# Attention with the value products turned over and GpSimd scaling the probabilities

## The reference

```
h = rms_norm(x, g)
proj = h @ w_in                            # queries, keys, values, gates
o_a = dilated_attention(...)               # 4 heads, 3 groups of keys under one softmax
o_b = sliding_window_gqa(...)              # 8 heads, softmax with a sink
o_c = stick_breaking_attention(...)        # 4 heads, no softmax
merged = g0*(o_a @ w_br_a) + g1*(o_b @ w_br_b) + g2*(o_c @ w_br_c)
x = x + rms_norm(merged @ w_out)
x = x + rms_norm(conv_ffn(rms_norm(x)))
# then, twice:
oa = neighbourhood_attention(...)          # 8 heads, softmax
ob = sliding_window_gqa_2(...)             # 8 heads, softmax with a sink
x = x + (g0*(oa @ w_branch_na) + g1*(ob @ w_branch_swa)) @ w_out
x = x + peer_ffn(rms_norm(x))              # 16 experts of 16384 for each of 8 heads
```

## Time and profile before

| | us |
|---|---|
| median of 3 runs | 2282.3 |
| lowest and highest | 2281.91, 2283.56 |
| span of the profiled execution | 2280.1 |
| PE busy | 2025.5 |
| DVE busy | 1598.8 |
| ACT busy | 1144.3 |
| POOL busy | 821.2 |

### The profile page before, as it was taken

One profiled execution on the slowest core, in us unless ns is written; L12 is line 12 of the kernel. 1 busy time (PEld: TensorE's weight loads), 2 busy tenths in 40 slices (PEclk: granted clock), 3 DMA queues, 4 the chain that ended last, 5 costly groups with the idle time before them and its releaser, 6 DMA issues.

```text
span 2280.1 us, 29665 instructions
## 1 busy us (share of the span) xinstructions
PE 2025.5 (89%) x9846; PEld 1333.5 (58%) x9846; DVE 1598.8 (70%) x3217; ACT 1144.3 (50%) x2531; POOL 821.2 (36%) x531
## 2 busy tenths in 40 slices
PE   9999999999999998888877878999999887778787
PEld 8998899998898744432222223898744432223222
DVE  4565777777676887777677765676887777677774
ACT  4454455555454555444444445454555544454443
POOL 0000000000010255565666663010256566765754
PEclk9999999999999999999999999999999999999999
DMA  7544456655735899999999997634899999999998
GB/s 244 168 122 131 137 163 186 191 180 149 235 120 163 329 421 421 421 421 421 420 421 422 419 422 318 230 121 148 320 421 421 421 421 422 421 422 411 422 422 339
DMA packets 120771, 707.22 MB, mean 310 GB/s; under 512 B 13664, under 2 KB 13920, under 8 KB 55008
## 3 DMA queue, kind: packets, MB, share of 16 engines
q0 software_dynamic: 73728, 536.90, 56.7%
q1 hardware_dynamic: 43488, 157.63, 21.8%
q10 hardware_dynamic: 3456, 11.40, 1.4%
HBM read 704.84 MB, written 1.05 MB: 310 GB/s over the span
## 4 chain that ended last, share of the span: by engine, by line
PE 40%; DMA 24%; POOL 11%; DVE 9%; issue 9%; ACT 7%; POOLq 0%; DVEq 0%; ACTq 0%
DMA work<-in_experts,expert_idx 23%; POOL work L1071 11%; PE ps L547 10%; PE ps L549 10%; PE ps L548 10%; PE ps L1296 6%; PE ps L697 2%; DVE weights_lo L532 2%; DVE work L2126 2%; PE ps L675 1%; ACT weights_hi L527 1%; ACT L1586 1%; ACT L1637 1%; PE ps L665 1%; DVE work L2103 1%
## 5 line engine op out<-in xcount | busy, mean ns | idle before, releaser
L1296 PE MATMUL ps<-work,arena 128*128 128x512 f32 x2040 | 995.2, 620 | 211.4 <-ACT arena L1642 210.6
L1071 POOL DMA_INDIRECT work<-in_experts,expert_idx x512 | 796.9, 1556 | 735.8 <-PE ps L1296 290.5
L1296 PEld LDWEIGHTS ps<-work,arena 128*128 128x128 f32 x2040 | 360.5, 192 | 820.1 <-ACT arena L1642 524.5
L2126 DVE CUSTOM_DVE_ANT_0 work<-h_norm,work 128x1024 f32<-128x1024 f32 x480 | 588.2, 1226 | 332.6 <-DMA work<-in_experts,expert_idx 328.8
L532 DVE TENSOR_TENSOR weights_lo<-weights,weights_hi 128x1024 fp32r<-128x1024 f32 x280 | 347.4, 1246 | 183.0 <-ACT weights_hi L527 181.8
L547 PE MATMUL ps<-feat_hi,weights_hi 128*128 128x256 f32 x1576 | 459.4, 291 | 8.7 <-DVE weights_lo L532 5.8
L1637 ACT ACTIVATE small<-small 128x1 f32<-128x1 f32 x512 | 150.3, 293 | 609.2 <-DVE small L2126 587.2
L527 ACT ACTIVATE weights_hi<-weights 128x1024 fp32r<-128x1024 f32 x280 | 295.3, 1056 | 316.2 <-PE ps L549 271.0
L548 PE MATMUL ps<-feat_lo,weights_hi 128*128 128x256 f32 x1576 | 446.7, 283 | 0.0
L549 PE MATMUL ps<-feat_hi,weights_lo 128*128 128x256 f32 x1576 | 446.7, 283 | 0.0
L547 PEld LDWEIGHTS ps<-feat_hi,weights_hi 128*128 128x128 f32 x1576 | 302.9, 192 | 18.4 <-issue 8.5
(11 more groups left out here) (242 smaller groups left out, 1760.3 us busy)
## 6 DMA issues: line engine op xcount, KB each, us to landing
weights<-in_wstream SPq DMA_DIRECT2D x280, 512.0 KB, 4.2
work<-in_experts,expert_idx POOLq DMA_INDIRECT x512, 14.6
arena<-in_wstream SPq DMA_DIRECT2D x12, 512.0 KB, 5.7
arena<-in_na_bias ACTq DMA_DIRECT2D x6, 512.0 KB, 4.1
params<-in_wstream SPq DMA_DIRECT2D x6, 512.0 KB, 5.4
arena<-in_bias ACTq DMA_DIRECT2D x5, 512.0 KB, 4.4
params<-in_par ACTq DMA_DIRECT2D x2, 576.0 KB, 5.6
params<-in_par ACTq DMA_DIRECT2D x1, 1024.0 KB, 6.2
```

The source lines that it names most:

```text
L1071: nc.gpsimd.indirect_dma_start(ring[:, r, :], None, experts, bass.IndirectOffsetOnAxis(ap=EIDX[:, b, c * RING + r:c * RING + r + 1], axis= ...
L1296: ins = nc.tensor.matmul(bank(2 * t + h), DIAG[:, r, :], ring[:, r, D + h * 512:D + (h + 1) * 512], start=False, stop=False)
L2126: nc.vector.tensor_tensor_reduce(ring[:, r, 0:D], HN[:, t, :], ring[:, r, 0:D], 1.0, 0.0, ALU.mult, ALU.add, hd[:, r:r + 1]).then_inc(dots ...
```

## The change

Value products are turned over: the 64 columns of values are stationary and 128 columns of transposed probabilities move. The result is feature-major, 64 rows for a head; the even head of a pair goes to partitions 0 to 63, the odd one to 64 to 127, alternating. O becomes OT, feature-major, and the turns of heads go. Of the batches before the last two, DVE copies the heads to OT, and ACT and DVE make FH and FL from OT at "O" (three pairs of chunks in the first block, two in a layer). For the last two batches ACT and DVE make FH and FL from PSUM.

Not the heads are scaled but the probabilities, before they are transposed: at the new step "N" (for a batch and a half) DVE waits for the exponentials of that half and takes the reciprocals of the sums, and GpSimd multiplies the half in place. PE's transposes wait for GpSimd's halves. The order becomes N(b-1, 0), S(b), V(b-2), N(b-1, 1), G, T, G, T. In the last steps a product of the branches ("F") moves ahead of the last transposes, and ACT's sigmoid of the gates moves to the place of "F", ahead of the last batch's heads. The diff's core:

```diff
-        O, w0 = carve(work, w0, TT, D)
+        OT, w0 = carve(work, w0, KC, S)
...
+            far = (min(4 * fills[-1] + 4, b.blocks) - 1) // per >= b.n // 2
+            pe.wait_ge(A.probs, 2 * (l * A.batches + b.at) + (2 if far else 1))
+            transposes_pe(pe, A, b.fill, [b.L[:, r, k * P:(k + 1) * P] for r in range(b.n) for k in range(per)], l, fills)
...
-            pe.wait_ge(A.pTt, l * A.fills + b.fill + b.copies)
             out = bank(4 + b.values % 2)
-            for r, (_, vals) in enumerate(b.rows):
-                for k, v in enumerate(vals):
-                    ins = nc.tensor.matmul(out[:, r * HD:(r + 1) * HD], PT[:, r * per + k, :], v,
-                                           start=k == 0, stop=k == per - 1)
+            for j in range(b.n // 2):
+                pe.wait_ge(A.pTt, l * A.fills + b.fill + max(b.copies - 1, -(-(2 * j + 2) * per // 4)))
+                for k in range(per):
+                    for side in range(2):
+                        r = 2 * j + side
+                        ins = nc.tensor.matmul(out[side * HD:(side + 1) * HD, j * P:(j + 1) * P], b.rows[r][1][k], PT[:, r * per + k, :],
+                                               start=k == 0, stop=k == per - 1)
...
-            if half:
-                ins.then_inc(A.probs, 1)
+            ins.then_inc(exps_ready, 1)
+
+        def normed_dve(dve, ch, A, b, half, l=0):
+
+            if b.kind != "softmax":
+                return
+            r0, r1 = half * b.n // 2, (half + 1) * b.n // 2
+            dve.wait_ge(exps_ready, A.soft_before + 2 * (l * A.batches + b.at) + half + 1)
+            nc.vector.reciprocal(rsum[b.turn][:, r0:r1], sums[b.turn][:, r0:r1]).then_inc(inverse_ready, 1)
+
+        def normed_pool(pool, A, b, l=0):
+
+            if b.kind != "softmax":
+                return
+            for half in range(2):
+                r0, r1 = half * b.n // 2, (half + 1) * b.n // 2
+                part = b.L[:, r0:r1, 0:b.width]
+                wait_alone(pool, inverse_ready, A.soft_before + 2 * (l * A.batches + b.at) + half + 1, pool_passed)
+                nc.gpsimd.tensor_tensor(part, part, view(rsum[b.turn][:, r0:r1], [1, r1 - r0], [0, b.width]), ALU.mult).then_inc(A.probs, 1)
...
-            if b.kind == "softmax" and fills[0] == 0:
-                ch.step(nc.vector.reciprocal(rsum[b.turn][:, 0:b.n], sums[b.turn][:, 0:b.n]))
+
+        def heads_of(b):
+
+            return slice(b.col // P, b.col // P + b.n // 2), slice(b.q * P, (b.q + 1) * P)
+
+        def heads_out(b):
+
+            return bank(4 + b.values % 2)[:, 0:b.n * HD].rearrange("p (c n) -> p c n", n=P)
+
+        def heads_act(act, A, b, l=0):
+
+            act.wait_ge(A.pTr, l * A.fills + b.values + 1)
+            nc.scalar.activation(FH[:, *heads_of(b)], heads_out(b), ACT.Copy).then_inc(heads_hi, 1)
 
         def heads_dve(dve, ch, A, b, l=0):
-            n = b.values
-            dve.wait_ge(A.pTr, l * A.fills + n + 1)
-            dst, src = O[:, b.q, b.col:b.col + b.n * HD], bank(4 + n % 2)[:, 0:b.n * HD]
-            if b.kind == "softmax":
-                ch.sync()
-                nc.vector.tensor_tensor(dst.rearrange("p (n d) -> p n d", n=b.n), src.rearrange("p (n d) -> p n d", n=b.n),
-                                        view(rsum[b.turn], [1, b.n], [0, HD]), ALU.mult).then_inc(A.pTt, 1)
+
+            if b.direct:
+                dve.wait_ge(heads_hi, A.hi_before + l * (A.early + 2) + A.early + b.direct)
+                nc.vector.tensor_tensor(FL[:, *heads_of(b)], heads_out(b), FH[:, *heads_of(b)], ALU.subtract).then_inc(A.pTt, 1)
             else:
-                nc.vector.tensor_copy(dst, src).then_inc(A.pTt, 1)
+                dve.wait_ge(A.pTr, l * A.fills + b.values + 1)
+                nc.vector.tensor_copy(OT[:, *heads_of(b)], heads_out(b)).then_inc(A.pTt, 1)
...
+        def straight(batches):
+
+            batches[-2].direct, batches[-1].direct = 1, 2
+
+        def heads_parts(eng, A, b, l=0):
+
+            for f in range(A.early):
                 if eng is nc.scalar:
-                    eng.wait_ge(A.pTr, l * A.fills + n + 1)
-                    nc.scalar.activation(two(FH, f), src, ACT.Copy).then_inc(heads_hi, 1)
+                    eng.wait_ge(A.pTt, l * A.fills + b.fill)
+                    nc.scalar.activation(two(FH, f), two(OT, f), ACT.Copy).then_inc(heads_hi, 1)
                 else:
-                    eng.wait_ge(heads_hi, l * 4 + (0 if A is AT1 else 4) + f + 1)
-                    nc.vector.tensor_tensor(two(FL, f), src, two(FH, f), ALU.subtract).then_inc(A.pTt, 1)
-
...
-        def early_heads_pe(pe, A, b, taken, l=0):
-
-            pe.wait_ge(*taken)
-            pe.wait_ge(A.pTt, l * A.fills + b.fill)
-            turn_heads(pe, A, b.fill + b.fills, l, range(EARLY))
+                    eng.wait_ge(heads_hi, A.hi_before + l * (A.early + 2) + f + 1)
+                    nc.vector.tensor_tensor(two(FL, f), two(OT, f), two(FH, f), ALU.subtract).then_inc(heads_lo, 1)
...
+                past = batches[b.at - 1]
+                order += [("N", past, 0), ("S", b)] + ([("V", batches[b.at - 2])] if b.at > 1 else []) + [("N", past, 1)] + turned(past)
+            return order + [("N", batches[-1], 0)]
...
-            return [("V", b), ("O", b), ("T", last, range(last.copies)), ("P", b), ("V", last)]
+            c = last.copies
+            middle = [("T", last, range(1, c - 1))] if c > 2 else []
+            return [("N", last, 1), ("O", b), ("V", b), ("T", last, range(1)), ("P", b)] + middle + [("F", b), ("T", last, range(c - 1, c)), ("V", last)]
...
+            for b in batches1:
+                normed_pool(pool, AT1, b)
...
+                for b in batches2:
+                    normed_pool(pool, AT2, b, l)
...
-            gates_act(3 * KC, (proj_taken, IN_QKV + IN_GATE))
+                elif what[0] == "F":
+                    gates_act(3 * KC, (proj_taken, IN_QKV + IN_GATE))
+                elif what[0] == "V" and what[1].direct:
+                    heads_act(act, AT1, what[1])
...
-                if what[0] in "GSP":
+                if what[0] in "GSO":
```

More of the change, by code:

```diff
@@ L68 @@
 QKW = QK_HEADS * HD
-EARLY = 2
 ROWS = 4
@@ L608, in build, with __init__ @@
         class Attn:
-            def __init__(self, low, scores, logits, probs, pTr, pTt, batches, fills):
-                self.low, self.scores, self.logits, self.probs = low, scores, logits, probs
+            def __init__(self, low, scores, logits, soft_before, probs, pTr, pTt, batches, fills, early, hi_before, lo_before):
+                self.low, self.scores, self.logits, self.soft_before, self.probs = low, scores, logits, soft_before, probs
+                self.early, self.hi_before, self.lo_before = early, hi_before, lo_before
                 self.pTr, self.pTt = pTr, pTt
@@ L764, in stick_dve @@
             mask = before[:, S - w:S]
-            nc.vector.tensor_tensor(b3, b3, view(mask, [0, b.n], [1, w]), ALU.mult).then_inc(A.probs, 1)
-        def heads_first(batches):
-            batches[-1].behind_heads = True
-            batches[-1].fill += EARLY
-            batches[-1].values += EARLY
-        def heads_parts(eng, A, fill, l, fills):
-            for f in fills:
-                n = fill + f
-                src = bank(6 + f if f < EARLY else 4 + n % 2)
+            dve.wait_ge(A.probs, 2 * b.at)
@@ L815, in branches_pe @@
         def branches_pe(pe, A, fill, g0, parts, l=0, at=0):
-            pe.wait_ge(A.pTt, l * A.fills + fill + EARLY)
-            turn_heads(pe, A, fill, l, range(EARLY, 4))
-            first_branch(pe, 2 * g0 + 2, 3, 0, parts[0], at)
-            pe.wait_ge(A.pTt, l * A.fills + fill + 4)
+            pe.wait_ge(heads_lo, A.lo_before + (l + 1) * A.early)
+            pe.wait_ge(A.pTt, l * A.fills + fill)
             for g in range(BR):
@@ L996, in build @@
         rest2 = attention(batches2)
-        order2 += rest2[:2] + [("Q", 1, range(0, 2)), ("Q", 1, range(2, 3))] + rest2[2:] + last_steps(batches2)
+        behind = rest2.index("G") + 1
+        order2 += rest2[:behind] + [("Q", 1, range(0, 2)), ("Q", 1, range(2, 3))] + rest2[behind:] + last_steps(batches2)
         assert order2.count("G") == L_PROJ + L_GATE
@@ L1566, in _ @@
                     elif what[0] == "O":
-                        heads_parts(nc.scalar, AT2, what[1].fill + what[1].fills, l, range(EARLY))
-                gates_act(2 * KC, (lproj_taken, l * N2 + L_PROJ + L_GATE))
+                        heads_parts(nc.scalar, AT2, what[1], l)
+                    elif what[0] == "F":
+                        gates_act(2 * KC, (lproj_taken, l * N2 + L_PROJ + L_GATE))
+                    elif what[0] == "V" and what[1].direct:
+                        heads_act(act, AT2, what[1], l)
                 merge_act(act, AT2, fill_o2, G_LAYER + LG_BR, l, at)
@@ L1721, in _ @@
                 elif what[0] == "O":
-                    heads_parts(nc.vector, AT1, what[1].fill + what[1].fills, 0, range(EARLY))
```

(9 more changed lines are left out.)

58 lines of the change are left out of this document (24 added, 34 removed).

## The result

| | before | after |
|---|---|---|
| median of 5 runs, us | 2282.87 | 2265.74 |
| lowest and highest | 2281.91, 2283.56 | 2264.86, 2269.29 |
| span of the profiled execution | 2280.1 | 2263.9 |

The ratio is 0.9927, with a 95% interval of 0.9914 to 0.9939. That is faster by 17.1 us; by the two spans it is 16.2 us. The forecast was 2267.

What follows compares the result with a forecast made beforehand. PE was taken to bound attention's steady part, a chain through DVE and ACT its tails. -14.0 + 1.4 + 0.7 - 2.4 - 1.1 = -15.4 us from 2280.1, plus 2.2 around the span, gave 2267 us; own range 2262 to 2277.

Steps and rivals of the forecast that it cites:

- the forecast's first three terms: Attention's steady part: value products -14.0 us, mode changes +1.4 and the slackless place +0.7.
- Value products, -14.0: Steady attention: two products side by side in the array's halves save 0.0565 us for each of 248 records, 14.0 us.
- Mode changes, +1.4: Nine steady batches of values between row-tiled scores and full-height products: 0.15 us each, bounds 0 to 0.35, +1.4 us.
- Slackless place, +0.7: After a layer's first scores PE waits for DVE's copies; extra reciprocal and contention add 0.35 us, +0.7 for two layers.
- GpSimd's half, 2.5 us: GpSimd's multiplication of half a batch, at most 128 x 1024, takes 2.5 us, upper end 4.1; hidden in the steady part.
- Layer tails, -1.2 each: Each layer's tail: first product needing all heads at 706.7 instead of 707.87 us, 1.2 us earlier, -2.4 for two.
- First block: Its tail, ending behind ACT's sigmoid: -1.1 us; its narrowest half, 512 elements, ready some 0.5 us before PE's transposes.
- the second rival: The array's halves take turns in the value products: 2284.5 us, or 2281 without mode changes; chance 0.17.
- GpSimd's contention costs in the steady part: Rival: DVE's splits behind GpSimd's 26 halves overrun their 3.5 us of slack, +17 us, 2299; chance 0.10.
- The loads of 64 columns: Rival: loads can't run ahead while the other half works, a record takes 0.276 us, +65, near 2345; chance 0.04.
- a mean above 1.25 us: Sign of the forecast: DVE's splits take a mean above 1.25 us, without a wait of PE in the steady part.
- the wait for GpSimd takes all of it: Layer's tail: the early branch starts where it did before, since the wait for GpSimd takes the saved turns and values.

Runs made afterwards that it cites:

- e1: The changed kernel with a batch's value products issued for all even heads first, then all odd ones, instead of alternating; 2276.75 us, 0.9976 of the kernel before.
- e3: The changed kernel with DVE multiplying the probabilities directly after its reciprocals, and GpSimd doing none of it; 2269.33 us, 0.9934 of the kernel before.
- e5: The changed kernel with the last batch's first half scaled one group earlier, the second behind the early heads' low parts; 2256.07 us, 0.9878 of the kernel before.
- e8: The changed kernel with each GpSimd multiplication followed by a second one of the same size by ones; 2269.71 us, 0.9946 of the kernel before.
- e4: The changed kernel with 7 and 9 matmuls of zeros in PE's two idle spells of each layer's tail; 2263.03 us, 0.9905 of the kernel before.
- e2: The changed kernel with GpSimd multiplying only 8 columns of each row, most probabilities left unscaled; 2253.65 us, 0.9871 of the kernel before.
- e6: The changed kernel with the first block's sigmoid of the gates cut up and mostly done during the projections; 2266.15 us, 0.9919 of the kernel before.
- e7: The changed kernel with both e5's scaling order and e6's early gates; 2254.96 us, 0.9873 of the kernel before.

## Why the prediction was right

The total was right, and so was its main part, the saving of PE in the steady part. Part of the agreement is luck. Measured in the traces, the steady parts gave -13.4 us (-5.3, -3.3, -4.8) where the forecast's first three terms make -11.9; the tails gave -4.3 (-1.5, -1.3, -1.5) for -3.5; and 1.5 us was lost again between and behind the attention stages, for which the forecast had no term. Inside these sums some smaller terms were mis-sized.

- **Value products, -14.0: right.** It took the half-cost from the scores' rows. The batch of 32 took 1.97 us against "near 1.9", and 18.93 became 17.26 us against 17.2. The saving per batch is 1.82 us, 0.0569 a record for 0.0565. e1 shows the mechanism: without alternation the batch takes 3.33. The Trainium skill, TensorEngine Tiling (Array Packing), section Tiling Modes, says that tiles execute independently, and here the trace agrees for tiles of 64 columns.
- **Mode changes, +1.4: right within its bounds.** From the last value record to the first product is 0.20 us, 0.12 more than before; from scores to values it is what it was (0.33 of waiting). Nine times 0.12 is 1.1 us.
- **Slackless place, +0.7: nothing was lost.** PE's waits there are 0.50 and 0.19 us, as before (0.49 and 0.19). The extra reciprocal and the contention fell on time that DVE had. e3 shows that the place is as slackless as I took it: 2.46 us of work added ahead of the copies made a wait longer by 2.46.
- **GpSimd's half, 2.5 us: too long.** Undisturbed it takes 1.90 us. Two of e5's and e8's rows show it (1.89, 1.90). The group lists 2.58 because of the time it waited behind DVE:

```profile
L743 POOL TENSOR_TENSOR work<-work,small 128x1024 f32<-128x1024 f32 x18 | 46.3, 2578 | 81.9 <-DVE small L733 81.9
```

  So 2.5 us against the listed 2.58 looks like a hit and isn't one. I had carried the rotary rows' 1.5 us for 640 elements over by length, 2.4 us. The two operations aren't alike: the rotary one reads two large inputs, this one a number for each row. Whether that is the reason, no run shows.
- **Layer tails, -1.2 each: -1.3 and -1.45, by two errors that cancel.** The turns between GpSimd and DVE were as forecast, but each was shorter, and PE's two idle spells were 1.68 and 2.22 us for 2.8 and 3.3, so the early branch started 2 us sooner than forecast; the clock's fall, which I had kept only for the upper end of the range, took back 1.5 to 1.7 us. The forecast ended at the right time for a partly wrong reason. e4 shows the fall's price, e5 the price of the turns and the fall together.
- **First block.** Its steady part gave -5.3 where my terms make 120 x 0.0565 - 5 x 0.15 = 6.0. The missing 0.7 is the batch whose halves are 512 elements, the one that I had called the narrowest place with 0.5 us to spare. PE, GpSimd and DVE there:

```profile
145.18 1.09 PE L676 MATMUL ps<-consts,work 128*128 128x128 f32 x8 [0.50 <-POOL work L743]
...
143.25 1.88 POOL L743 TENSOR_TENSOR work<-work,small 128x512 f32<-128x512 f32 x1 [5.01 <-DVE small L733]
...
142.90 0.17 DVE L733 RECIPROCAL small<-small 128x4 f32<-128x4 f32 x1
143.00 1.23 DVE L532 TENSOR_TENSOR weights_lo<-weights,weights_hi 128x1024 fp32r<-128x1024 f32 x1
```

  The step that failed is "by the order of the code it is ready some 0.5 us before": PE waited 0.50 us for it instead. I counted the half alone. DVE's next instruction is a split with both inputs in SBUF, so GpSimd stood 0.9 us behind it before its own 1.0. In the layers' tails I had made GpSimd wait behind a split; here I had not. e2 and e3, where GpSimd has next to nothing or nothing to multiply, show the 0.7: from score batch to score batch around this place they take 15.95 us, the changed kernel 16.66. The block's tail gave -1.5 for -1.1; the sigmoid ends the wait, as forecast. The fall of the clock behind that wait (0.50 over 212.0 to 215.4 us) was not in the forecast, which had falls in the layers' tails alone; the kernel before had its own at 242 us, and from the end of the tail to layer 1's first stage 0.4 us is lost in all.
- **The rivals.** That the halves take turns is refuted by the batch of 1.97 us; in e1, where they do, it takes 3.33. Two sums of theirs had slips: without mode changes the second rival gives 2284.5 - 1.4 = 2283, not 2281, and the forecast's own upper end holds one fall of the clock, where two make 2278.6. That GpSimd's contention costs in the steady part is refuted in the layers (e8: twice the work, the same period) and true only for the first block. The loads of 64 columns did not hold a record to its 0.276 us: 32 of them fit in the 1.97 us.
- **DVE's splits "a mean above 1.25 us": 1.258 against 1.246.** The trace agrees, and it says little, since most splits lie in other stages.

The 9.7 us that e5 found were in view from the forecast itself. I had written that "the wait for GpSimd takes all of it" in the tail, and treated it as a price of the change. It was a price of two lines of its order, the fall of the clock included.

## What to carry to other kernels

If a product has 64 columns on one side, try that side as the stationary one, and issue the two halves of the array in alternation; the order alone was worth 1.36 us in a batch of 32 records here. Where work goes to GpSimd, ask at each place which DVE instruction with both inputs in SBUF will stand beside it, in both directions, for each of the two can make the other late. And at the end of a stage, look at the order before you look at the engine: the same multiplication cost 5 us a layer in one place, 1.5 of them by the clock that fell, and nothing when one half came two steps earlier and the other one step later.

## What the runs showed of the hardware

- **A copy of eight numbers waits for GpSimd.** The copy of the sinks, SBUF to SBUF with one input, is listed in the kernel before and then in the changed one:

```profile
L703 DVE COPY work<-params 128x8 f32<-128x8 f32 x6 | 1.0, 170 | 0.0
```

```profile
L708 DVE COPY work<-params 128x8 f32<-128x8 f32 x6 | 9.9, 1653 | 0.0
```

  Its mean went from 0.17 to 1.65 us, ten times. GpSimd is the cause: in e3, where it multiplies nothing, the mean is 0.168 us, and in e2, with 8 columns, 0.207. The logits of these batches start up to 1.7 us later; in a layer nothing waits for them. The Trainium skill, SBUF — State Buffer, section Who interferes with whom, says that copies can enter a mode that uses the port shared with GpSimd, and the trace agrees. I had counted only DVE instructions with two inputs.
- **The turns are whole instructions.** Where halves of GpSimd's and low parts of DVE's stand beside each other, each low part waits for a whole half: 0.65 us of work is listed at 2.34, in e8 too.
- **A record with 64 stationary columns costs 0.103 us alone**, 0.0635 side by side, and 0.119 with 128 stationary and 64 moving columns.
- **Where the clock falls isn't fixed by the idle spell before it.** In the changed kernel it fell at 212 and 686.5 us, behind idle spells of 2.27 us and of 1.68 and 2.22. Behind the spell of 2.05 us at 205.7 it did not fall, and in e4, with the same instructions and the same spell, it did. Between e6 and e7, with spells of 2.57 and 2.56 us at one place, only e6 fell. What decides stays open; each trace shows one execution, so part of this can differ from one execution of a kernel to the next.
- **A fall avoided at one place can come at another.** Before, it fell at some 242 and 768 us (granted 0.91 over 760 to 780); after, 760 to 780 has 1.00. In e5, without idle spells in the layers' tails, and in e4, with filled ones, a fall is at 740 to 760 (0.91). It need not cost there what it cost in a tail: e4 kept the gain of its tails, 2260.8 us of span for 2263.9.
